# Narrow projection tiles with tokens stationary, and a new order of the first attention, in a two-block transformer kernel

## What is computed

```
h = rms_norm(x, attn_norm)
z = h @ w_in                    # conv input, q (12 heads), 6 key/value parts, g (36 columns)
gates = sigmoid(g)              # 3 gates for each token and head
kc, vc = compress(...)          # keys and values of 16-token strides, through silu
o_c = softmax(q kc) vc; o_s = softmax(q ks) vs; o_w = softmax(q kw) vw
nsa = gate0 * o_c + gate1 * o_s + gate2 * o_w
x = x + concat(conv_out, nsa) @ w_out
```

## Time and profile before

| what | value |
|---|---|
| median of 3 runs | 737.0 us (736.04 to 737.31) |
| the profiled execution's own time | 736.97 us |
| its span, first to last instruction | 735.1 us |
| PE busy | 98% of the span, 5430 matmuls and as many weight loads |
| DVE, ACT, POOL busy | 73%, 53%, 5% |
| mean granted clock of TensorE | 0.995 of full speed |

### The profile page before, as it was taken

One profiled execution on the slowest core, in us unless ns is written; L12 is line 12 of the kernel. 1 busy time (PEld: TensorE's weight loads), 2 busy tenths in 40 slices (PEclk: granted clock), 3 DMA queues, 4 the chain that ended last, 5 costly groups with the idle time before them and its releaser, 6 DMA issues.

```text
span 735.1 us, 13433 instructions
## 1 busy us (share of the span) xinstructions
PE 721.5 (98%) x5430; PEld 664.1 (90%) x5430; DVE 536.3 (73%) x935; ACT 388.9 (53%) x567; POOL 37.6 (5%) x53
## 2 busy tenths in 40 slices
PE   7999999999999999999999999999999999999996
PEld 7999987799999999988999989999888899999995
DVE  6798898676767777758569979995877885455554
ACT  7655999463344433447255457676446435445442
POOL 2700000000000000000532000000000000000000
PEclk9999999999999999999999999999999999999999
DMA  9746611678888778631554447454813774554511
GB/s 328 247 135 227 225 56 59 252 308 311 323 314 323 301 290 309 229 121 57 184 182 175 173 158 300 174 200 169 319 57 115 284 264 155 212 182 169 220 58 58
DMA packets 27024, 151.12 MB, mean 206 GB/s; under 512 B 3129, under 2 KB 7837, under 8 KB 9565
## 3 DMA queue, kind: packets, MB, share of 16 engines
q1 hardware_dynamic: 22620, 124.81, 46.7%
q10 hardware_dynamic: 3456, 25.17, 8.7%
q0 software_dynamic: 896, 0.43, 0.3%
HBM read 148.92 MB, written 1.05 MB: 204 GB/s over the span
## 4 chain that ended last, share of the span: by engine, by line
PE 84%; DVE 10%; ACT 3%; issue 1%; DMA 1%; SPq 0%; DVEq 0%; ACTq 0%
PE ps L464 25%; PE ps L465 24%; PE ps L466 24%; DVE w_lo L1820 3%; PE ps L860 2%; PE ps L598 1%; PE ps L622 1%; DVE misc L2333 1%; PE ps L582 1%; PE ps L1115 1%; DVE misc L2327 1%; DVE small L2332 1%; DMA raw<-rows_b 1%; PE ps L653 1%; PE ps L635 1%
## 5 line engine op out<-in xcount | busy, mean ns | idle before, releaser
L1820 DVE TENSOR_TENSOR w_lo<-raw,w_hi 128x2048 fp32r<-128x2048 f32 (+2 forms) x105 | 237.0, 2262 | 99.3 <-ACT w_hi L1294 99.1
L464 PE MATMUL ps<-h_hi,w_hi 128*128 128x256 f32 (+2 forms) x984 | 279.8, 284 | 0.0
L465 PE MATMUL ps<-h_lo,w_hi 128*128 128x256 f32 (+2 forms) x984 | 278.3, 283 | 0.0
L466 PE MATMUL ps<-h_hi,w_lo 128*128 128x256 f32 (+2 forms) x984 | 278.3, 283 | 0.0
L1294 ACT CAST w_hi<-raw 128x2048 fp32r<-128x2048 f32 (+2 forms) x105 | 197.0, 1888 | 49.4 <-PE ps L466 45.5
L464 PEld LDWEIGHTS ps<-h_hi,w_hi 128*128 128x128 f32 (+2 forms) x984 | 187.2, 190 | 2.5 <-issue 1.3
L465 PEld LDWEIGHTS ps<-h_lo,w_hi 128*128 128x128 f32 (+2 forms) x984 | 187.2, 190 | 1.1
L466 PEld LDWEIGHTS ps<-h_hi,w_lo 128*128 128x128 f32 (+2 forms) x984 | 187.2, 190 | 0.3
L464 PE MATMUL ps<-w_hi,mix_hi 128*128 128x512 f32 x248 | 97.6, 394 | 0.6 <-DVE small L1965 0.4
L465 PE MATMUL ps<-w_lo,mix_hi 128*128 128x512 f32 x248 | 96.8, 390 | 0.0
L466 PE MATMUL ps<-w_hi,mix_lo 128*128 128x512 f32 x248 | 96.5, 389 | 0.0
(11 more groups left out here) (326 smaller groups left out, 891.3 us busy)
## 6 DMA issues: line engine op xcount, KB each, us to landing
raw<-wts SPq DMA_DIRECT2D x109, 1024.0 KB, 4.8
ada<-w_ada ACTq DMA_DIRECT2D x24, 1024.0 KB, 5.2
alibi<-wts SPq DMA_DIRECT2D x2, 1024.0 KB, 6.0
fa_whole<-wts SPq DMA_DIRECT2D x2, 1024.0 KB, 5.8
resid<-x SPq DMA_DIRECT2D x2, 512.0 KB, 3.8
raw<-wts SPq DMA_DIRECT2D x2, 512.0 KB, 6.6
rows_ga<-rows_wide SPq DMA_DIRECT2D x1, 1024.0 KB, 8.4
out<-resid SPq DMA_DIRECT2D x4, 256.0 KB, 2.0
```

Of the source, the lines that this page charges most:

```text
L464: nc.tensor.matmul(o, lh, rh, start=start, stop=False)
L465: nc.tensor.matmul(o, lh, rl, start=False, stop=False)
L466: return nc.tensor.matmul(o, ll, rh, start=False, stop=stop)
L1820: V.tensor_tensor(w_lo[:, s % RING, 0:w], raw[:, n_of[name] % RAW, 0:w], w_hi[:, s % RING, 0:w].bitcast(F32), ALU.subtract).then_inc(w_rea ...
```

## The change

It does four things. (1) Both narrow tiles hold 128 tokens stationary and stream 36 or 8 weight columns, for two token halves: 48 matmuls each in place of 24, and the result already has tokens on partitions; the copies and the two pairs of transposes go, and ACT reads the result once. (2) In the first attention the gate tile comes first on PE and its sigmoid first on ACT, the four compressor parts stand nearly in a row, score pair 2, cmp_keys, half of vw, values(2) and the turns 7 and 8 change place. (3) ACT and DVE lists are rewritten to match: the two silus together, splits later, scalings (`normal`) between the masks (`masked`), several waits on `p_ready` and `p_exp` dropped. (4) In the second attention 7 instead of 3 chunks stand in front of `scores_a(0)`.

```diff
@@ narrow tiles @@
-            def narrow_tile(slot, o, a, n, cols):
+            def narrow_rows(slot, o, a, n, cols):
 
                 wh, wl = w3(slot, DC, DC * cols)
-                for k in range(DC):
-                    i = mm3(o, wh[:, k, a:a + n], wl[:, k, a:a + n], h_hi[:, k, :], h_lo[:, k, :], k == 0, k == DC - 1)
+                for m in range(2):
+                    ms = slice(m * P, (m + 1) * P)
+                    for k in range(DC):
+                        i = mm3(o(m), h_hi[:, k, ms], h_lo[:, k, ms], wh[:, k, a:a + n], wl[:, k, a:a + n], k == 0, k == DC - 1)
                 return i
...
-                narrow_tile(slot, ps[0:G_COLS, bank, 0:T], 0, G_COLS, G_COLS).then_inc(pe_tile, 1)
+                narrow_rows(slot, lambda m: ps[:, bank, T + m * HD:T + m * HD + G_COLS], 0, G_COLS, G_COLS).then_inc(pe_tile, 1)
...
-            def gate_turn():
-
-                pe.wait_ge(narrow_sb, 1)
-                for m in range(2):
-                    i = nc.tensor.transpose(ps[:, 7, T + m * HD:T + m * HD + G_COLS], gT[:, m * P:(m + 1) * P], ident[0:G_COLS, 0:G_COLS])
-                i.then_inc(narrow_ps, 1)
...
@@ first attention, TensorE @@
+            gate_tile()
             compress(0, 0)
-            compress(0, 1)
             pe.wait_ge(z_evac, s_idx["k0"] + 1)
             scores(0)
-            gate_tile()
+            compress(0, 1)
+            compress(1, 0)
             conv_mean_row()
+            compress(1, 1)
             pe.wait_ge(s_sb, 8)
             scores(1)
-            compress(1, 0)
-            cmp_keys()
-            compress(1, 1)
             pe.wait_ge(convd_ready, 1)
             vs_at = own_bank("vs")
             token_half(*vs_at, 0)
+            cmp_keys()
             conv_var_columns()
             cmp_values()
-            gate_turn()
             pe.wait_ge(lnv_ready, 1)
             token_half(*vs_at, 1).then_inc(pe_tile, 1)
+            pe.wait_ge(s_sb, 16)
+            scores(2)
             cmp_scores()
             pe.wait_ge(z_evac, s_idx["g"] + 1)
             vw_at = own_bank("vw")
             token_half(*vw_at, 0)
-            token_half(*vw_at, 1).then_inc(pe_tile, 1)
             pe.wait_ge(sc_sb, 1)
             probs_turn(0)
-            pe.wait_ge(s_sb, 16)
-            scores(2)
+            token_half(*vw_at, 1).then_inc(pe_tile, 1)
             probs_turn(1)
...
             probs_turn(6)
+            values(2)
+            probs_turn(7)
             pe.wait_ge(s_sb, 40)
             scores(5)
-            probs_turn(7)
-            values(2)
+            probs_turn(8)
             values(3)
-            probs_turn(8)
...
@@ second projections and second attention, TensorE @@
-            narrow_tile(slot, ps[0:NB_HEADS, bank, T:2 * T], P, NB_HEADS, IDX_COLS).then_inc(pe_tile, 1)
+            narrow_rows(slot, lambda m: ps[:, 7, m * NB_HEADS:(m + 1) * NB_HEADS], P, NB_HEADS, IDX_COLS).then_inc(pe_tile, 1)
...
             feature_2("qi0")
-            pe.wait_ge(narrow_sb, 2)
-            for m in range(2):
-                i = nc.tensor.transpose(ps[:, 7, m * NB_HEADS:(m + 1) * NB_HEADS], wiT[:, m * P:(m + 1) * P], ident[0:NB_HEADS, 0:NB_HEADS])
-            i.then_inc(narrow_ps, 1)
             feature_2("qi1")
...
-            gate_half(0, 0, 0, 3)
+            gate_half(0, 0, 0, 7)
             scores_a(0)
-            gate_half(0, 0, 3)
+            gate_half(0, 0, 7)
...
@@ first attention, ScalarE @@
-            nc.scalar.preload_act_table_set("silu_and_others")
+            gates_out()
+            nc.scalar.preload_act_table_set("exp_and_others")
+            attn(0)
             act.wait_ge(direct_done, 2)
             nc.scalar.copy(xs_cmp(0), ps[:, 4, 0:264]).then_inc(cmp_sb, 1)
-            cmp_silu(0)
-            attn(0)
             attn(1)
-            after(7)
             act.wait_ge(direct_done, 4)
             nc.scalar.copy(xs_cmp(1), ps[:, 5, 0:264]).then_inc(cmp_sb, 1)
-            copy_out(s_idx["g"])
+            cmp_silu(0)
             cmp_silu(1)
-            cmp_keys_out()
-            gates_out()
-            after(8)
+            after(7)
             act.wait_ge(lnv_ready, 1)
             nc.scalar.activation(lncol[:, 2:4], lncol[:, 0:2], ACT.Sqrt).then_inc(lnsq_ready, 1)
-            act.wait_ge(p_ready, 4)
             attn(2)
-            after(9)
-            copy_out(s_idx["vs"])
-            act.wait_ge(p_ready, 8)
+            cmp_keys_out()
+            after(8)
             attn(3)
             act.wait_ge(sc_sb, 1)
             nc.scalar.activation(scmp, scmp, ACT.Exp).then_inc(pc_exp, 1)
+            copy_out(s_idx["vs"])
+            after(9)
             turned_out(0)
...
@@ first attention, VectorE @@
-            compressor_sum(0)
             masked(0)
             masked(1)
-            dve.wait_ge(p_exp, 4)
+            dve.wait_ge(z_evac, s_idx["g"] + 1)
+            normal(0)
+            conv_less_mean()
+            compressor_sum(0)
+            compressor_sum(1)
+            normal(1)
             masked(2)
-            conv_less_mean()
-            dve.wait_ge(p_exp, 8)
             masked(3)
...
```

More of the change, by code:

```diff
@@ L181, in build @@
         pcmp = early[:, 2748:3516].rearrange("p (m h n) -> p m h n", m=2, h=NQ)
-        gT = early[0:G_COLS, 3516:3772]
-        wiT = misc[0:NB_HEADS, 1536:1792]
         probs = [soft[:, 0:768], soft[:, 768:1536], rows_ga[:, 0, 0:768], rows_ga[:, 1, 0:768]]
@@ L276, in build @@
         lnr_ready, lnrow_ps = sem("lnr_ready"), sem("lnrow_ps")
-        narrow_sb, narrow_ps, wi_ready = sem("narrow_sb"), sem("narrow_ps"), sem("wi_ready")
+        wi_ready = sem("wi_ready")
         sc_ps, sc_sb, pc_exp, pc_ready, pcT_ps, pcT_ready = (sem(n) for n in (
@@ L1357, in copy_out @@
                     nc.scalar.copy(zt(U)[:, 1, :], ps[:, 3, 0:T]).then_inc(z_evac, 1)
-                elif name == "g":
-                    nc.scalar.copy(gT, ps[0:G_COLS, bank, 0:T]).then_inc(narrow_sb, 1)
                 elif name == "v":
@@ L1416, in gates_out @@
             def gates_out():
-                act.wait_ge(narrow_ps, 1)
+                act.wait_ge(pe_tile, s_idx["g"] + 1)
                 nc.scalar.activation(gates, ps[:, 7, T:T + 2 * HD].rearrange("p (m c) -> p m c", m=2)[:, :, 0:G_COLS].rearrange(
@@ L1473, in _ @@
             turned_out(2)
-            act.wait_ge(p_ready, 16)
             attn(5)
@@ L1478, in _ @@
             turned_out(4)
+            keep_mix(0)
+            turned_out(5)
             act.wait_ge(p_ready, 24)
             attn(7)
-            turned_out(5)
-            keep_mix(0)
             keep_mix(1)
@@ L1486, in _ @@
             turned_out(7)
-            act.wait_ge(p_ready, 32)
             attn(9)
-            keep_mix(2)
             attn(10)
             turned_out(8)
+            keep_mix(2)
             after(s_idx["vw"])
-            keep_mix(3)
             turned_out(9)
@@ L1496, in _ @@
             attn(11)
+            keep_mix(3)
             turned_out(10)
+            keep_mix(4)
             after(s_idx["k1"])
-            keep_mix(4)
             turned_out(11)
@@ L1646, in _ @@
                 if name == "idx":
-                    nc.scalar.copy(wiT, ps[0:NB_HEADS, bank, T:2 * T]).then_inc(narrow_sb, 1)
+                    nc.scalar.copy(wi_s, ps[:, 7, 0:2 * NB_HEADS].rearrange("p (m h) -> p m h", m=2)).then_inc(wi_ready, 1)
                     nc.scalar.copy(kiT, ps[:, bank, 0:T]).then_inc(z_evac, 1)
@@ L1656, in _ @@
                     nc.scalar.mul(dst, src, scale).then_inc(z_evac, 1)
-                if name == "qi0":
-                    act.wait_ge(narrow_ps, 2)
-                    nc.scalar.copy(wi_s, ps[:, 7, 0:2 * NB_HEADS].rearrange("p (m h) -> p m h", m=2)).then_inc(wi_ready, 1)
                 if name == "vb0":
@@ L2053, in conv_lo @@
                     V.tensor_tensor(mix_lo[:, c, :], conv[:, c, :], mix_hi[:, c, :].bitcast(F32), ALU.subtract).then_inc(clo_ready, 1)
-            compressor_sum(0)
             masked(0)
             masked(1)
-            dve.wait_ge(p_exp, 4)
+            dve.wait_ge(z_evac, s_idx["g"] + 1)
[4 more added lines that the diff above has]
+            normal(1)
             masked(2)
-            conv_less_mean()
-            dve.wait_ge(p_exp, 8)
             masked(3)
-            compressor_sum(1)
-            after(7)
             variance_columns()
             cmp_values_out()
-            dve.wait_ge(z_evac, s_idx["g"] + 1)
-            normal(0)
+            after(7)
+            root_columns()
+            normal(2)
+            cmp_scores_out()
             after(8)
-            cmp_scores_out()
-            normal(1)
-            root_columns()
-            after(9)
+            dve.wait_ge(pT_ps, 2)
+            masked(4)
             cmp_probs_out()
             normalised()
-            normal(2)
-            dve.wait_ge(pT_ps, 2)
-            masked(4)
+            normal(3)
             dve.wait_ge(pT_ps, 4)
-            dve.wait_ge(p_exp, 16)
             masked(5)
```

(15 more changed lines are left out.)

## The result

The change makes the kernel slower: 747.66 us (median of 5 executions, 746.48 to 749.22) against 736.45 for the kernel before on the same chip, a ratio of 1.0146 with a 95% interval of 1.013 to 1.0163. The forecast was 740.7, with 738.6 to 743.6 as its range. The direction was right and the size was not: it cost 11.2 us where 3.7 were expected. The profiled execution took 746.48 us, 9.5 more than that of before, with a span of 744.6 us.

The account below looks back on a forecast made before the run. PE was taken as the bound, with a matmul in flight for 98% of the span. Terms +2.5 +2.5 -0.4 -0.4 -0.2 -0.3 = +3.7 us on 737.0 gave 740.7 us, range 738.6 to 743.6.

Parts of the forecast that it names:

- Loads of the narrow tiles: Gate and idx tiles: 48 load-paced matmuls at 0.111 us, 5.3 us a tile, +2.5 us each, +5.0 together.
- the one-column and the 64-column rows: Variance columns (line 684) and compressed values (line 705): 0.111 and 0.113 us a matmul, so the load sets the pace.
- Rival 1: Narrow tiles: loads cheaper, 0.06 us a matmul, giving 735.8 us, or 731 with loads wholly hidden; chance 0.10.
- rival 4: Both narrow tiles: few streamed columns lower TensorE's clock, losing 2.7 to 5.3 us, 743.4 to 746; chance 0.05.
- in `idx` loads never stop: At the idx tile: the argument given against TensorE's clock falling there; no size of its own.
- The order of the first attention: First attention, new lists: masks come sooner, k1 wait stays; -0.2 us, bounds -1.1 to +2.
- only waits can change: First attention: every piece of PE work is kept, so the new order can only alter PE's waits; term -0.2 us.
- sign of being wrong: At out0_part: PE arriving less than 1 us or more than 4 us later than before would show the prediction wrong.
- Rival 2: First attention, cmp_scores: a late split on ACT makes PE wait, losing 0.9 us or more, say 742.5; chance 0.13.
- The waits kept and moved: scores(3) still waits about 0.7 us for ACT's copy; scores_a(0) stops waiting; turn_a(0) waits some 0.8 us for DVE.
- The second attention: Four more chunks before scores_a(0) fill its 1.0 us wait, but turn_a(0) then waits for DVE: gain 0.3 us.
- Transposes and `idx`: Removed transpose pairs save 0.4 us at gates and 0.4 at idx; delay at idx counted in full to the end.

Follow-up runs that it names:

- f3: The changed kernel with 128 columns streamed in every matmul of both narrow tiles, in place of 36 or 8: 743.4 us, ratio 1.0077.
- e1: The kernel before with only its two narrow tiles turned round (48 matmuls each, no copies or transposes), old order: 750.1 us, ratio 1.0181.
- e3: The changed kernel with each narrow-tile matmul streaming 256 columns in place of 36 or 8, the extra sums unread: 744.5 us, ratio 1.0101.
- e4: The changed kernel with DVE's nsa_lo(3) and nsa_lo(4) put back in front of the splits of k1 and out0: 749.1 us, ratio 1.0164.
- e2: The changed kernel with the narrow tiles, copies and transposes of before; new order and seven chunks kept: 739.0 us, ratio 1.003.
- e5: The changed kernel with the old narrow tiles and transposes, and nsa_lo(3), nsa_lo(4) back in front of the splits: 737.75 us, ratio 1.0004.
- e6: The changed kernel with narrow tiles streaming 256 columns, and nsa_lo(3), nsa_lo(4) back in front of the splits: 743.1 us, ratio 1.008.
- e8: The kernel before with only seven chunks in place of three in front of scores_a(0) in the second attention: 737.25 us, ratio 1.0.
- f1: The changed kernel with the idx tile, its copy and its two transposes as before; gate tile stays turned round: 743.8 us, ratio 1.009.
- e7: The changed kernel with the narrow matmuls at idx placed between the wide ones (256, 8, 8 columns in turn), gates as changed: 750.9 us, ratio 1.0178.
- f2: The changed kernel with the second token half of each narrow tile streaming 256 columns, the first still 36 or 8: 745.9 us, ratio 1.0106.
- g1: The kernel before with one line moved, so that ACT copies k1 ahead of attn(4): 740.4 us, ratio 1.0036.

## Why the prediction missed

**Loads of the narrow tiles: right.** The step from the one-column and the 64-column rows to 0.111 us a matmul held for 36, for 8 and (f3) for 128 columns, and the tiles took 5.36 and 5.38 us where 5.3 were forecast. Rival 1, cheaper loads, is refuted by the 0.11. The Trainium skill ("TensorE: Matmul & The Clock Gate", "Back-to-back issue gap") gives about 81 ns for a sustained stream at 128 columns; here it is 0.11 us with 128 columns too (f3).

**The clock: wrong, and the larger part of the miss.** The failed step is the sentence that spoke against rival 4, "in `idx` loads never stop". It took a full record of PE for activity. The clock falls within 0.2 us of the end of both tiles, although PE and PEld never pause in them (e1: inside them). In e3 and f3, with the same loads and 256 or 128 columns streamed, it does not fall. The Trainium skill ("TensorE: Matmul & The Clock Gate", "Part 1: The HAM clock gate") says that the clock follows how busy PE has recently been; in these runs a full record of loads and matmuls did not hold it. Rival 4 priced its fall at 2.7 to 5.3 us, worked out for the tiles themselves. The price was about right, the place was not: in the change the tile is hardly touched and the successor pays, 3.4 us for both places in the profile. In e1 and e4, where the falls begin inside the tiles, the loss is 6.8 for both. With 3.4 the forecast would have been 744.1, and with the order as measured (below) 746.6.

**The order of the first attention: wrong in sign.** Its term was -0.2, and from trace to trace it measures 0.6 + 0.3 + 1.4 = +2.3 (e2, which also holds the second attention, has +2.2 in all). The step that failed is "only waits can change", followed by a search for waits in the pieces that the prediction had picked out, ACT's copies and the masks. 1.4 of the 2.3 is a wait, and the other 0.9 is mostly small steps between groups, which no wait shows; they had no term in the sum. The prediction's own sign of being wrong was met: PE reaches `out0_part` 4.7 us later than before (115.37 and 120.05), with 4 as the bound. For the wait, the full diff shows `nsa_lo(3)` and `nsa_lo(4)` moving behind the splits `after(k1)` and `after(out0)` on DVE, and the prediction never asked who needs them. `values(5)` does. The timeline of DVE and PE in the changed kernel, 126 to 137 us:

```profile
126.72 1.01 DVE L1957 TENSOR_SCALAR rows_ga<-rows_ga,small 128x128 f32<-128x128 f32 x4
131.18 2.29 DVE L1798 TENSOR_TENSOR w_lo<-raw,w_hi 128x2048 fp32r<-128x2048 f32 x1 [3.46 <-ACT w_hi L1282]
133.75 2.29 DVE L1798 TENSOR_TENSOR w_lo<-raw,w_hi 128x2048 fp32r<-128x2048 f32 x1 [0.27 <-ACT w_hi L1282]
135.96 0.75 DVE L1961 TENSOR_TENSOR mix_lo<-ps,mix_hi 128x256 fp32r<-128x256 f32 x2
...
136.43 0.65 PE L646 MATMUL ps<-misc 128*64 128x256 f32 x4 [1.31 <-DVE mix_lo L1961]
```

DVE stands idle for 3.5 us waiting for a split of ACT, while a step of 0.4 us that PE will need is queued behind it. Putting it back removes the wait (e5, e6). Rival 2 had the right mechanism, a split ahead of something PE needs, its sum of 0.9 us or more, and the wrong place, `cmp_scores`. That place shows no wait in the profile after. What is left of the order, 0.3 us in e5 with an interval of -0.4 to +1.0, is beyond what the totals resolve; the small steps stand in the profiles alone.

**The waits kept and moved: right.** `scores(3)` waits 0.7 for ACT's copy, and `turn_a(0)` waits 0.7 for DVE where 0.8 was named. The second attention gains 0.2 in e8 where 0.3 was forecast, and 0.2 in the change (9.7 us behind the kernel before ahead of it, 9.5 at `turn_a(0)`).

**Transposes and `idx`: right.** From `cmp_values` to the token half behind it PE takes 0.4 us, where it took 0.8 with the transposes between. The delay at `idx` reached the end in full, as f1 shows.

The sum, redone with what was measured in the profiles: +5.0 loads, -0.8 transposes, +3.4 clock, +2.3 order, -0.2 second attention and -0.2 not traced = +9.5. Of the 11.2 of the medians, 0.5 is the profiled execution of before lying above its median, and 1.2 the profiled execution of after lying below its own, which stays open.

## What to carry to other kernels

When an edit swaps few full-width matmuls for many that stream little, price its loads from the nearest rows and then ask what the clock will do: the end of the tile and its successor pay, and widening the moving operand under a load that sets the pace anyway can be free (36 and 8 columns made 128: ratio 1.0077 in place of 1.0146). When a list is reordered, go through every instruction that moved behind a wait, however small, and name its consumer; the wait to look for is that of the engine in front of it, not its own length. And judge an edit of 1 us only in kernels whose clock is steady: e4 seemed to lose what e5 and e6 show it gains.

## What was not expected of the hardware

- Behind or inside 48 loads and matmuls 0.11 us apart without a pause, with 8 or 36 columns streamed, the granted clock fell to the 1.2 GHz level in every profile that has such a row of 48 (the change, e1, e4, e7 and f1). With 128 or 256 columns at the same places it stayed at 1.00 (e3, e6, f3).
- Alternating steps of 256, 8 and 8 columns was no better than 48 narrow ones in a row: in the profiles 10.2 us at the lower level at `idx`, not 3.4.
- The fall at the gates lasted 3.4 us in the profiles of the change and f1 and 6.8 in those of e4 and e7, though the four programs are the same up to there. The totals of kernels with falls spread by 1.5 to 4.6 us (the change, e1, e4, e7, f1, f2), those of e2, e3, e5, e6 and f3 by 1 to 1.5. But e8 and the kernel before spread by up to 2.4 without a fall at these places, so a wide spread alone shows none.
- Behind a wait of PE of 2.2 us came a fall that lasted 3.4 us (g1, one profile); the wait of 1.3 at `values(5)` in e2 and the change brought none.
